# Prompt attention placed between the convolution tiles of a hybrid decoder kernel, with the residual parked in HBM

## The reference

```
p = rmsnorm(x) @ w_in                      # one projection for both head groups
q, k = silu(causal_conv(mq, mk)); h = mlstm_chunkwise(q, k * 128**-0.5, mv, gates)   # 4 heads of 128
a = softmax attention over indexer-selected keys (8 query heads, 4 key heads of 64; top 128 of
    the prompt's keys, top 256 of a sample's 1028)
x = x + concat(h, a) @ w_out
x = x + (silu(g) * u) @ w_down, with g, u = rmsnorm(x) @ w_gate_up
```

## Time and profile before

| | us |
|---|---|
| median of 3 runs | 2268.02 (2266.82 to 2275.93) |
| the profiled execution | 2275.45 |
| its span, first to last instruction | 2273.7 |
| TensorE busy | 2085.8 (mean granted clock 0.887) |
| VectorE busy | 1129.1 |
| ScalarE busy | 432.0 |
| POOL busy | 309.6 |

### The profile page before, as it was taken

How to read it: one execution, slowest core, us unless ns; L and a number is a source line. 1 busy time by engine, 2 the same in 40 slices (tenths; PEclk the granted TensorE clock), 3 DMA queues, 4 the chain that set the end, 5 groups by cost and what they waited for, 6 DMA issues and landing times. The chain is left out here.

```text
span 2273.7 us, 30865 instructions
## 1 busy us (share of the span) xinstructions
PE 2085.8 (92%) x11906; PEld 1678.4 (74%) x11906; DVE 1129.1 (50%) x2114; ACT 432.0 (19%) x922; POOL 309.6 (14%) x272
## 2 busy tenths in 40 slices
PE   5999978799998999999969999688999989999998
PEld 4775575566467999989957656655654779999898
DVE  3375995727203333345425669965470053333553
ACT  2123211332201000031021322223332010000400
POOL 2452342100000000000026423420000000000000
PEclk8898995855998999999969999877569989999999
DMA  3220311141302223223122212112323113223231
GB/s 114 75 77 9 114 38 40 42 143 48 112 32 74 75 75 109 77 61 94 52 63 77 75 32 91 45 33 88 103 66 121 37 37 106 81 75 100 58 97 65
DMA packets 193708, 165.37 MB, mean 73 GB/s; under 512 B 30882, under 2 KB 173506, under 8 KB 193554
## 3 DMA queue, kind: packets, MB, share of 16 engines
q1 hardware_dynamic: 193554, 163.32, 23.2%
HBM read 153.57 MB, written 9.71 MB: 72 GB/s over the span
## 5 line engine op out<-in xcount | busy, mean ns | idle before, releaser
L1033 PE MATMUL psum<-x_high,w_split_even 128*128 128x272 f32 x1408 | 248.7, 295 | 13.3 <-DVE x_low L1827 13.3
L1033 PE MATMUL psum<-x_high,w_split_odd 128*128 128x272 f32 x1408 | 237.6, 288 | 0.0
L1033 PEld LDWEIGHTS psum<-x_high,w_split_even 128*128 128x128 f32 x1408 | 206.4, 194 | 18.2 <-issue 18.2
L1014 PE MATMUL psum<-h_high,w_split_even 128*128 128x272 f32 x1232 | 204.6, 287 | 1.7 <-issue 1.7
L1033 PEld LDWEIGHTS psum<-x_high,w_split_odd 128*128 128x128 f32 x1408 | 199.5, 188 | 0.0
L1851 DVE TENSOR_TENSOR proj<-rawr,psum 128x544 f32<-128x544 f32 x44 | 31.7, 721 | 332.8 <-PE psum L1033 332.8
L1014 PEld LDWEIGHTS psum<-h_high,w_split_even 128*128 128x128 f32 x1232 | 173.4, 188 | 2.5 <-issue 2.5
L970 PE MATMUL psum<-h_high,x_high 128*128 128x512 f32 (+1 forms) x400 | 169.7, 424 | 1.5 <-ACT proj L732 1.5
L970 PE MATMUL psum<-h_high,x_low 128*128 128x512 f32 (+1 forms) x400 | 163.5, 409 | 0.0
L970 PE MATMUL psum<-ring_low,x_high 128*128 128x512 f32 (+1 forms) x400 | 162.5, 406 | 0.0
L613 POOL TENSOR_TENSOR ring_low<-ring,h_high 128x512 fp32r<-128x512 f32 (+1 forms) x96 | 157.4, 1640 | 7.7
(11 more groups left out here) (363 smaller groups left out, 3607.1 us busy)
## 6 DMA issues: line engine op xcount, KB each, us to landing
ring<-in_w_gate_up_dram SPq DMA_DIRECT2D x44, 1024.0 KB, 7.1
ring<-in_w_in_dram SPq DMA_DIRECT2D x14, 2048.0 KB, 8.1
ring<-in_w_down_dram SPq DMA_DIRECT2D x16, 1408.0 KB, 6.9
ring<-in_w_out_dram SPq DMA_DIRECT2D x4, 2048.0 KB, 7.7
ring<-in_cache_k_dram SPq DMA_DIRECT2D x48, 128.0 KB, 2.0
cq<-in_cache_k_dram SPq DMA_DIRECT2D x48, 128.0 KB, 2.0
R<-in_cache_kidx_dram SPq DMA_DIRECT2D x128, 32.0 KB, 1.7
cq<-in_state_C_dram SPq DMA_DIRECT2D x16, 256.0 KB
```

Source lines behind the costliest of these rows:

```text
L1014: mm = pe.matmul(out[:, 512 * hf:512 * hf + HALF], down_part(c, w)[:, cols], v[:, HALF * hf:HALF * hf + HALF], start=(k == 0 and q == 0), ...
L1033: mm = pe.matmul(out[:, 512 * hf:512 * hf + HALF], w_part(f, w)[:, k, u, :], v[:, k, HALF * hf:HALF * hf + HALF], start=(k == 0 and q == 0 ...
```

## The change

It does the following.

- The 32 steps of prompt attention leave their stage. Five of them (`AP_STEPS`) stand inside each convolution tile 2 to 7, behind K chunks 1, 3, 4, 6 and 7; steps 30 and 31 and the drain stand behind tile 7. In `prompt_step(n)` TensorE issues the scores of step n, the values of n-3 (`AP_LAG`) and the transposes of n-2. Values use one bank, `ps(7)`, transposes one, `ps(6)`.
- q and k are turned inside tile 1 in six groups instead of eight: the heads of q are stored in another order, so k needs no doubled copy.
- On ScalarE a tile's five exponentials and copies come first, with the silu of tile m-2 behind the third of them, and then the reading of tile m. On VectorE the taps of tile m-1 stand behind the first and the second maximum and one sample pick behind the fourth.
- The taps run over the whole row of 568 columns, prompt and samples in one operation. `raw` has three buffers for eight tiles. POOL copies the tails.
- Turned k and the first convolved rows lie in `x`. So `x` is stored to HBM (`x_spill`) after the first norm, and loaded back after the attention rows have been turned.
- k isn't scaled by POOL; the factor goes into gate columns and into the mLSTM's score products.
- Picks: 6 beside the convolution as before, 4 behind the last attention step, 8 in the mLSTM, and so 14 after mixing.
- Values of request 1 and keys of request 5 load early. After the stores SP loads requests 2 and 3, values of 0, `x`, request 4, values of 5.
- The attention rows are written into `qk` and are turned (`turn_out`) around the turning of the mLSTM heads.

```diff
-        cqv = qk2[:, :].rearrange("p (k t) -> p k t", k=KT)
+        x_spill = nc.dram_tensor("x_spill", (P, KT * T), F32).ap()
+
+        def conv_place(m):
+            return (x, 2048 + CONV_ROW * m) if m < MH else (qk2, 2048 + CONV_ROW * (m - MH))
+
+        def conv_row(m):
+            buf, at = conv_place(m)
+            return buf[:, at:at + CONV_ROW]
...
+        a_score = R4[:, 0:1536].rearrange("p (s c) -> p s c", s=3)
+        a_pt = (R4[:, 1536:2048], kiT[:, :])
...
+                sp.wait_ge(s_rstd1, 1)
+                sp.dma_start(x_spill, x[:, :]).then_inc(s_x_spilled, 16)
...
-                load_pages(1, ("cache_k",))
+                load_pages(1, ("cache_k", "cache_v"))
+                load_pages(5, ("cache_k",))
...
-                sp.wait_ge(s_mix_turned, MH)
                 load_both(2)
                 load_both(3)
                 load_pages(0, ("cache_v",))
-                load_pages(1, ("cache_v",))
-
-                sp.wait_ge(s_qt_turned, 8)
+                sp.wait_ge(s_x_spilled, 16)
+                sp.wait_ge(s_a_turned, 4)
+                sp.dma_start(x[:, :], x_spill).then_inc(s_x_back, 16)
                 load_both(4)
-                sp.wait_ge(s_a_s, 4 * QH)
-                load_both(5)
-
+                load_pages(5, ("cache_v",))
                 sp.wait_ge(s_kt_turned, 4)
                 load_pages(7, ("cache_k",))
...
-                for m in range(MH, 2 * MH):
-                    pool.wait_ge(s_conv_silu, m + 1)
-                    pool.tensor_scalar(cqv[:, m, :], cqv[:, m, :], P ** -0.5, None, ALU.mult).then_inc(s_k_scaled, 1)
...
+                    row, new = conv_row(m), conv_samples(m)
+                    act.activation(row[:, 0:SEQ], row[:, 0:SEQ], ACT.Silu)
+                    act.activation(row[:, SEQ:T].rearrange("p (b t) -> p b t", b=DB), new, ACT.Silu).then_inc(s_conv_silu, 1)
+
+                def read_conv(m):
+
+                    src = slot(CONV0 + m).rearrange("p (h t) -> p h t", h=2)
+                    if m == 0:
+                        act.wait_ge(s_qk_ready, 1)
+                    if m >= 3:
+                        act.wait_ge(s_conv_z, m - 2)
+                        act.wait_ge(s_conv_done, m - 2)
...
+                def prompt_probs(n):
+
+                    if n < 4 * QH:
+                        j, h = n // QH, n % QH
+                        w = (j + 1) * P
+                        act.wait_ge(s_a_max, n + 1)
+                        if h == 0 and j >= 2:
+                            act.wait_ge(s_a_tok, j - 1)
+                        act.activation(a_score[:, n % 3, 0:w], a_score[:, n % 3, 0:w], ACT.Exp, bias=a_neg[:, n % 4:n % 4 + 1],
+                                       scale=HD ** -0.5, accum_out=a_sum[:, j % 2, h:h + 1]).then_inc(s_a_p, 1)
+                    m = n - (AP_LAG - 1)
+                    if 0 <= m < 4 * QH:
+                        w = (m // QH + 1) * P
+                        act.wait_ge(s_pt_turned, m + 1)
+                        if m >= 2:
+                            act.wait_ge(s_pv, m - 1)
+                        act.activation(a_pt[m % 2][:, 0:w], ps(6)[:, 0:w], ACT.Copy).then_inc(s_pt_copied, 1)
...
+                read_conv(0)
+                act.wait_ge(s_x_spilled, 16)
+                for g in range(6):
+                    act.wait_ge(s_qt_turned, g + 1)
+                    act.activation(qT[:, g, :] if g < 4 else kT2[:, g - 4, :], ps(4 + 2 * (g % 2)), ACT.Copy).then_inc(s_qt_copied, 1)
+                read_conv(1)
+                for m in range(2, 8):
+                    for n in range(AP_STEPS * (m - 2), AP_STEPS * (m - 1)):
+                        prompt_probs(n)
+                        if n == AP_STEPS * (m - 2) + 2:
+                            conv_silu(m - 2)
+                    read_conv(m)
+                for n in range(AP_STEPS * 6, 4 * QH + AP_LAG):
+                    prompt_probs(n)
...
+                conv_tile(1, lambda k: turn_pair(k) if k < 6 else None)
...
+                def prompt_step(n):
+
+                    if n == 0:
+                        pe.wait_ge(s_sscore_copied, 1)
+                    if n < 4 * QH:
+                        j, h = n // QH, n % QH
+                        q0, g = HD * (h // 2 % 2), 2 * (h // 4) + h % 2
+                        if n >= 2:
+                            pe.wait_ge(s_a_max, n - 1)
+                        pe.matmul(ps(4 + n % 2)[:, 0:(j + 1) * P], qT[q0:q0 + HD, g, P * j:P * j + P],
+                                  kT2[q0:q0 + HD, h // 4, 0:(j + 1) * P], start=True, stop=True).then_inc(s_a_s, 1)
+                    m = n - AP_LAG
+                    if 0 <= m < 4 * QH:
+                        j, h = m // QH, m % QH
+                        pe.wait_ge(s_pt_copied, m + 1)
+                        if h == 0 and j >= 1:
+                            pe.wait_ge(s_a_tok, j)
+                        for s in range(j + 1):
+                            mm = pe.matmul(ps(7)[:, HD * h:HD * h + HD], a_pt[m % 2][:, P * s:P * s + P],
+                                           va[:, s, HD * (h // 2):HD * (h // 2) + HD], start=(s == 0), stop=(s == j))
+                        mm.then_inc(s_pv, 1)
+                    m = n - (AP_LAG - 1)
+                    if 0 <= m < 4 * QH:
+                        pe.wait_ge(s_a_p, m + 1)
+                        if m >= 1:
+                            pe.wait_ge(s_pt_copied, m)
+                        for s in range(m // QH + 1):
+                            mm = pe.transpose(ps(6)[:, P * s:P * s + P], a_score[:, m % 3, P * s:P * s + P], ident)
+                        mm.then_inc(s_pt_turned, 1)
+
+                after = {1: 0, 3: 1, 4: 2, 6: 3, 7: 4}
                 for m in range(2, 8):
-                    conv_tile(m)
+                    conv_tile(m, lambda k: prompt_step(AP_STEPS * (m - 2) + after[k]) if k in after else None)
+                for n in range(AP_STEPS * 6, 4 * QH + AP_LAG):
+                    prompt_step(n)
...
+                def taps(m, js):
+
+                    row, r_ = conv_row(m), raw[m]
+                    if js[0] == 0:
+                        dve.wait_ge(s_out_free, CONV0 + m + 1)
+                    for j in js:
                         w = vT[:, 8 * j + m:8 * j + m + 1]
-                        for out, src in ((cqv[:, m, 0:SEQ], r_[:, j:j + SEQ]), (seqs(cqv[:, m, :]), hist[:, :, j:j + DT])):
-                            if j == 0:
-                                ins = dve.tensor_scalar(out, src, w, None, ALU.mult)
-                            else:
-                                ins = dve.scalar_tensor_tensor(out=out, in0=src, scalar=w, in1=out, op0=ALU.mult, op1=ALU.add)
+                        if j == 0:
+                            ins = dve.tensor_scalar(row, r_[:, j:j + CONV_ROW], w, None, ALU.mult)
+                        else:
+                            ins = dve.scalar_tensor_tensor(out=row, in0=r_[:, j:j + CONV_ROW], scalar=w, in1=row, op0=ALU.mult, op1=ALU.add)
                         if j < 3:
                             step(ins)
-                    ins.then_inc(s_conv_z, 1)
-
-                    dve.tensor_copy(tails[:, 27 * m:27 * m + 3], r_[:, SEQ:SEQ + 3])
-                    dve.tensor_copy(tails[:, 27 * m + 3:27 * m + 27].rearrange("p (b j) -> p b j", b=DB), hist[:, :, 4:7]).then_inc(s_conv_done, 1)
-                    if m == 1:
-                        read_sample_scores()
-                    if m >= 8 - PICKS_CONV:
-                        pick_sample()
+                    if js[-1] == 3:
+                        ins.then_inc(s_conv_z, 1)
+
+                def prompt_max(n):
+
+                    if n < 4 * QH:
+                        j, h = n // QH, n % QH
+                        w = (j + 1) * P
+                        dve.wait_ge(s_a_s, n + 1)
+                        if n >= 3:
+                            dve.wait_ge(s_pt_turned, n - 2)
+                        mask = const("pen0") if j == 0 else penv[:, j - 1, 0:w]
+                        step(dve.tensor_tensor_reduce(a_score[:, n % 3, 0:w], ps(4 + n % 2)[:, 0:w], mask, 1.0, GONE, ALU.add, ALU.max,
+                                                      a_neg[:, 4 + n % 4:5 + n % 4]))
+                        dve.tensor_scalar(a_neg[:, n % 4:n % 4 + 1], a_neg[:, 4 + n % 4:5 + n % 4], -HD ** -0.5, None, ALU.mult)\
+                           .then_inc(s_a_max, 1)
+                    if n >= QH + AP_LAG and (n - AP_LAG) % QH == 0:
+                        j = (n - AP_LAG) // QH - 1
+                        dve.wait_ge(s_pv, QH * (j + 1))
+                        dve.wait_ge(s_a_p, QH * (j + 1))
+                        step(dve.reciprocal(a_sum[:, j % 2, :], a_sum[:, j % 2, :]))
+                        dve.tensor_tensor(qk[:, j, 0:QH, :], ps(7).rearrange("p (h d) -> p h d", h=QH),
+                                          a_sum[:, j % 2, :].unsqueeze(2).broadcast_to([P, QH, HD]), ALU.mult).then_inc(s_a_tok, 1)
+
```

(17 more changed lines are left out.)

236 lines of the change are left out of this document (82 added, 154 removed).

## The result

| | median us | range | against before |
|---|---|---|---|
| before | 2271.97 | 2266.82 to 2276.55 | |
| after | 2310.28 | 2301.89 to 2322.69 | 1.018 (95%: 1.0137 to 1.0223) |

The change makes the kernel slower by 38 us, 1.8%. I had forecast 2262, slightly faster than before. The range (2224 to 2312) holds the time only at its upper end, and the sign is wrong.

What follows compares the result with a forecast made beforehand. TensorE was taken as the bound, busy 92% of the span, with attention at half clock. Per layer 4 + 95 + 32 - 60.8 - 73 = -2.8 us, -5.6 in all, scaled to the median 2262 us; range 2224 to 2312.

Steps and rivals of the forecast that it cites:

- the sign: Whole kernel: slightly faster, -2.8 us per layer, -5.6 in all; chances faster 0.40, same 0.26, slower 0.34.
- Two terms of 70 us: Per layer: +70 us for pieces 1 to 3 against -73 us in sample attention, nearly cancelling.
- Piece 1: Turning of q and k in convolution tile 1: +4 us per layer, bounds 3 and 7.
- Piece 2: Convolution tiles 2 to 7 with 30 attention steps: 95 us per layer, bounds 76 and 118.
- The placement by hand: Steps of tiles 2 to 7 placed with waits on in-order queues: 90.8 us at full clock.
- third rival: Tiles 2 to 7: clock falls after waits of 2 to 3 us; stretch 118 us, kernel 2308 us; chance 0.22.
- Piece 3: Behind tile 7, drain, last normalisation, four picks, weighting and turning of k: 32 us, bounds 27 and 36.
- Piece 4: mLSTM stage and mixing: nothing saved by moving k's factor; sample attention starts 2.4 us sooner.
- Piece 5: Sample attention: prompt attention's 104.0 us go, but request 6's keys come late; -73 us, bounds -82 and -65.
- The fourth: Rival: table switch between exponentials costs 1.3 us more, twice per tile; kernel 2286 us; chance 0.06.
- second rival: Tiles 2 to 7: waits hide, the stretch is TensorE's 80 us; kernel 2228 us; chance 0.30.
- the fifth: Rival: attention steps don't overlap and run as before between the chunks; about 2340 us; chance 0.04.

Runs made afterwards that it cites:

- e13: Changed kernel with only filling added: matmuls whose results nobody reads, in five waits of the stretch of tiles 2 to 7; 2297.61 us, 1.01 of before.
- e12: e11 without the 12 filling matmuls ahead of state_C, so e7 plus three filled normalisation waits; 2197.41 us, 0.967 of before.
- e3: Changed kernel with SP loading the keys of requests 4, 6 and 7 ahead of the remaining values and the residual; 2267.15 us, 0.9966 of before.
- e11: e7 plus unread matmuls: 16 in each of three waits for a normalisation, 12 ahead of the first turning of state_C; 2211.96 us, 0.9714 of before.
- e8: Changed kernel with a silu's two parts in steps 2 and 3 of each tile instead of both in step 2; 2311.87 us, 1.0157 of before.
- e10: Changed kernel with 14 unread matmuls in the wait within tile 2's last attention step; 2310.98 us, 1.0162 of before.
- e1: Changed kernel with GpSimd's product of the output gate moved behind the last weighting of k; 2305.14 us, 1.0122 of before.
- e6: Changed kernel with tile 7's taps behind VectorE's work on the scores of steps 30 and 31; 2287.85 us, 1.0049 of before.
- e5: Changed kernel with the four picks ahead of VectorE's last normalisation instead of behind it; 2284.37 us, 1.0041 of before.
- e7: Changed kernel with the edits of e1, e3, e5 and e6, and all eight silus between the drain's copies; 2221.3 us, 0.9761 of before.
- e4: Kernel before the change with GpSimd's product of the output gate behind the last weighting of k; 2269.27 us, 0.9973 of before.

## Why the prediction was wrong, point by point

*The sum against its pieces.* Two terms of 70 us cancelled, and I said that the sign was weak. It fell because of four misses that all pointed the same way: the clock in the stretch, the drain, the turning behind it, and state_C with the mLSTM.

*Piece 1*, right: 2.6 us instead of 4, within the bounds.

*Piece 2, the stretch.* The placement by hand had the right waits (second layer of after: 6.3 us in three for normalisations, 4.3 for copies), and its sum was right to 0.3 us (e13). That closeness is part luck: tiles 2 to 7 of e13 take 12.0, 12.4, 15.5, 17.3, 16.2 and 17.7 us, so the first five were placed 2.2 us short and the last 1.8 long. What failed is the step to the clock. I took 4 us of loss by comparing with the indexer at 0.91. It was 17 and 6 us (108.1 and 97.1 less 91.1). The third rival is thus half of the answer: it named the mechanism, with 14 us at 1.2 GHz as the point where it decides; the first layer had about 45 us there (0.21 of 108.1, at half clock, twice), the second about 14. Its place, behind each wait, was right too. Its time of 2308 is near the measured one by coincidence only, since it rested on a stretch of 118. The reason that I gave with it, the transposes, does not hold: e12 has all of them and stays at 1.00, and so do the first 57.8 us of e3's first layer, without any filling. With the long waits filled no fall is left (e11 to e13), but not every wait brings one (e3). Why the fall in tile 2 of after lasts 3.4 us in one layer and 20.5 in the other is open; e8 to e10 did not settle it.

*Piece 3, the tail.* 41.8 us instead of 32, in both layers. Its steps: the drain took 26.8 instead of 19. Of these 7.8, 5.3 is GpSimd's product (e1). I had worked out that the taps stand ahead of the scores, but priced them at 2.75 us, from the undisturbed row. The trace of before had six such taps at 10.15 us beside a splitting operation and the same product, and I passed over it. The order explains the rest: with the scores ahead of the taps (e6) the drain takes 15.7 and 14.5 us, less than my 19. The turning took 15.1: 1.1 for the normalisation and 10.5 for the picks, as placed, and 3.5 for the weighting and turning behind them where I had taken 1.6. That the picks need not be on the path at all (e5) was in reach too: VectorE idles for 13.1 us in the drain.

*Piece 4, the mLSTM.* "Nothing" left out the clock behind the tail. state_C's turning and product keep TensorE busy all the time and took 20.0 and 16.9 us at clock 0.50 and 0.60, where before had 16.3 and 11.7 at 0.65 and 0.92; with the picks in the drain (e5) they took 12.5 and 16.3. The mLSTM itself took 78.6 and 74.5 us (74.5 and 74.0 before). The 2.4 us that were saved in mixing came as 1.6. That it is the lower clock is shown; why it is lower is open. The length of the pause ahead of it does not explain it, since before has the longer one:

```profile
1470.03 1.88 PE L1188 MATMUL psum<-con,tails 128*27 128x128 f32 x8 [18.07 <-DVE tails L1642]
```

In before, too, the clock falls while TensorE is busy with state_C, and its two layers differ there by 4.6 us, where the prediction took them as equal within 1 us. These are the second layer of before, then of after, each from the start of state_C:

```profile
1476.60:1486.40 9.80, 9.55 (x90) 9.31 (x88) 0.88 (x2) 4.59 (x8) 0.00 (x0) 1.00 0.40 117
1486.60:1488.34 1.74, 1.74 (x10) 1.72 (x9) 0.00 (x0) 1.18 (x1) 0.00 (x0) 0.50 0.28 92
...
1579.65:1581.50 1.85, 1.85 (x10) 1.62 (x9) 0.68 (x1) 0.60 (x1) 0.00 (x0) 0.50 0.53 164
1581.80:1585.00 3.20, 3.20 (x32) 3.20 (x32) 0.00 (x0) 1.59 (x3) 0.00 (x0) 1.00 0.51 168
1585.20:1596.51 11.31, 11.31 (x56) 11.29 (x54) 0.00 (x0) 3.67 (x5) 0.00 (x0) 0.50 0.45 131
```

*Piece 5, sample attention*, right: 73.2 us up to request 6's keys (72.2 and 1.8 of restart), with the wait of 9.8 ahead of them, and 52.6 behind. But I left a lead there. The waits of 4.1, 15.1 and 9.8 us came out of an order of issues, and I took the order as given. e3 shows it to be worth 24 us per layer, more than the loss.

*The other rivals.* The fourth, a dearer table switch, falls: a block from the first load to the exponential took 3.36 us (1448.30 to 1451.66), forecast 3.4, with 0.01 to 0.02 us between its operations, although a copy had just ended ahead of it. The Trainium skill (ScalarE: Activation LUTs, What ACT_TABLE_LOAD costs) charges a drain besides; this trace has none. The second rival's stretch of 80 us was never seen: 87.3 is the least, without blocks and at full clock. Its 80 is nearer to TensorE's own work than the 76 of the forecast: the 86.6 us busy in e12, less 48 filling products at an estimated 0.15 us (12 took 1.77 in e13), leave some 79.5. No row fits the fifth.

*What e7 and e12 say of the change.* The idea isn't what costs. The move with four other orders of the same work and the silus elsewhere gives 0.976, and with three filled waits 0.967. Of these edits only the later product (e4) was tried on the kernel before, which gains 0.3% from it; what filled waits or later silus would give there is not known.

## What to carry to other kernels

When a price is taken from one row, look at the longest row of the same instruction too, and at what ran on the other engines beside it. When work is moved out of a stretch, list what it was covering, then look whether the order of what stays exposed is free. And price a wait of TensorE with the clock behind it: in after, 8.4 and 10.6 us of short waits in the stretch were paid for at their own length and with 17 and 6 us of lower clock on top. One profile is not enough to know that price, since two layers with the same code differ by 11 us.

## What the runs showed of the hardware

**GpSimd holds up VectorE.** A tap of 128x568, whose two tensor inputs lie in SBUF, took up to 4.93 us beside a GpSimd product of 4.70, and 0.81 alone; the first tap, with one such input, 2.31 instead of 0.55 (e6). Not held up were VectorE's operations on scores, whose one large input is in PSUM (0.69 beside the product in e6), nor the selection rounds (in after, first layer, MATCH_REPLACE8 at 1.23 us within a GpSimd product of 1.89). The Trainium skill (SBUF — State Buffer, Who interferes with whom) states this: the two engines share a pair of SBUF ports, and a VectorE operation with two SBUF inputs, or one in a two-port mode as a scalar product can be, excludes a GpSimd operation that reads SBUF; the later one waits until the other is through. The rows agree.

**The clock.** Most waits of 1.3 to 2.6 us between dense work were followed by 1.2 GHz for 3.4 to 13.7 us, and the one in tile 2 for up to 23.9 (e3 and e6, in one layer each); some were followed by none (e3's first layer). Matmuls whose results nobody read, in the same waits, kept it at 2.4 GHz throughout (clock 1.00 in six stretches of six). In turnings and small products it can stay down although TensorE is never idle (19.98 us busy of 19.98 at 0.50), and it can fall there (from 1.00 to 0.50 within state_C, busy 3.20 of 3.20 and 11.31 of 11.31 us).

**SP's issuing.** With single pages at 1.1 us and pairs at 1.57, sample attention follows from adding up issues in both orders tried (after: 124.9 forecast, 124.7 and 125.8 measured; e3: 102 expected, 101.0 and 101.6 measured). The mean DMA share over the stage was at most 0.55.
